# Second block's attention: each unit's z quarter in two halves around the turn of the weights

## Chip, cores and metric

One core of a Trainium2 chip. The metric is the device time of one execution in microseconds; the kernel before took 2187.45 us (median of three runs, 2185.56 to 2187.83).

## What is computed

A hybrid layer with a gated feed-forward network, and behind it a second block. All is float32, in 1024 positions of 1024 channels. Cut to what matters here:

```python
proj = h @ w_in                                   # h: normalized rows; z is its last 1024 columns
a_u, a_v, sq, sk, sv, mq, z = jnp.split(proj, split_at, axis=-1)
y_a = chunked_spatial_gating(gelu(a_u), gelu(a_v), ...)
y_b = sliding_window_attention(sq, sk, sv, attn_sinks, rel_bias)   # 4 heads of 64, blocks of 128 queries, 256 keys
y_c = memory_cross_attention(mq, mk, mv)                           # 4 heads of 64, 256 memory keys
y = jnp.concatenate([y_a, y_b, y_c], axis=-1) * jax.nn.silu(z)
x = x + rms_norm_2(y @ w_out, post_norm_g)
```

## The kernel before

The kernel is written by hand: each engine has its own instruction stream in a fixed order, and the streams meet at semaphores. Every product is made of three matmuls, for each float32 operand is split into a high and a low part (hi·hi, hi·lo, lo·hi). ScalarE makes the high part by a copy, VectorE or POOL the low part by a subtraction.

The attention of the second block is a loop over 16 **units** (`UNITS2`, L636): for each of 8 blocks of 128 queries first the sliding window (kind 0, even units), then the memory (kind 1, odd units). TensorE does in it four things:

- `logits2(n)` (L1615): 12 small matmuls into banks 1 and 2 or 4 and 5. It runs three units ahead, and waits until the exponentials of unit n-2 are done.
- `turn2(n)` (L1633): eight 128x128 transposes (L1639) of the normalized weights `p_s` into banks 6 and 7. It waits for `pn_done`, VectorE's normalization of unit n.
- `z_quarter(n)` (L1658): the projection z of 128 channels for 256 positions, 8 channel blocks of three matmuls (L1670), summed in bank 0. It waits for the weights' low part (`wlo_done`) and for the z copy of unit n-1 (`zcopy_done`), which empties bank 0. Its last matmul raises `lin_full`.
- `values2(n)` (L1642): 12 matmuls (L1655) into bank 3. It waits for `p2lo_done`, both low parts of the turned weights, and for `pvg_done`, the product that took unit n-1's values out of bank 3.

ScalarE's order in unit n (L2404): p_hi, the high parts of the turned weights (L2409); then `exps2(n + 2)`, four exponentials and, in even units, a fifth small one on `se` (L2375, L2379); then `z_copied(n)` (L2402), the copy of bank 0 to `z_s`; in odd units the silu over `z_s` (L2418). Exponential and silu need different tables, so a table load comes with each change. Behind every fourth unit ScalarE splits the next z weights (`w_hi`, L1721), and POOL subtracts their low part in four pieces (L3616).

VectorE's order in unit n (L3214): `maxima(n + 2)` (L3156 to L3167: a scale and bias, a maximum, two small operations `mx` and `nm`); p_lo (L3222); `gated_values(n - 1)` (L3208: two products into yz); in even units `z_product` (L3200); `sink_share`; `normed(n + 1)` (L3184 to L3189), which writes `p_s`.

After the loop, `y_high(0)` (L2395) on ScalarE, queued behind the last z copy, and `y_low(0)` (L3212) on VectorE give the first operands of the output product (L1692).

```python
for n in range(len(UNITS2)):
    if n >= 1:
        values2(n - 1)
    turn2(n)
    z_quarter(n)
    if n + 3 < len(UNITS2):
        logits2(n + 3)
```

Of the kernel before, what the change touches and what calls it, by code (L numbers as in the profile page):

```python
# [23 lines left out]
KD = D // P  # L24
# [140 lines left out]
def build(nc, I, out, scratch):  # L165
    PANELS, TILES = linear_plan()
    PANEL_AT = {key: p for p, key in enumerate(PANELS)}
    TILE_AT = {key: n for n, key in enumerate(TILES)}

    THROUGH = {p: max(n for (key, _), n in TILE_AT.items() if key == PANELS[p]) + 1 for p in range(len(PANELS))}  # L170
    WIDTH = {"wa": 512, "wc": 512, "poolw": 512}

# [4 lines left out]
    AT2 = {key: PB2 + n for n, key in enumerate(PANELS2)}  # L177
    TICK2 = {key: L2 + n for n, key in enumerate(TICKS2)}
    THROUGH2 = {key: max(n for (k_, _), n in TICK2.items() if k_ == key) + 1 for key in PANELS2 if (key, 0) in TICK2}
    UP_AT = {key: n for n, key in enumerate(UPPER)}  # L180

# [41 lines left out]
    with ExitStack() as ctx:  # L223
# [9 lines left out]
        def sem(name):  # L233
            return ctx.enter_context(nc.semaphore(name))
# [219 lines left out]
        whi_done, wlo_done, lin_full, pair_full = sem("whi_done"), sem("wlo_done"), sem("lin_full"), sem("pair_full")  # L454
# [46 lines left out]
        def tile_rows(r):  # L501
            return P if r < 8 else META
# [4 lines left out]
                       for half in range(2)]  # L507

        SCORES_TO = [sum(blk <= b for blk, _, _, _ in SCORES) for b in range(NB)]

        def scores_behind(kind, m, j, half):
# [58 lines left out]
        zs_done, ZS_0 = gate_done, 4 * KD  # L570
        zcopy_done, ZCOPY_0 = y_done, 4 * KD
# [70 lines left out]
        def key_chunks(n):  # L642
            return [1] if n == 0 else [0, 1]
# [388 lines left out]
        def _(pe):  # L1032
# [106 lines left out]
            for r in range(NB):  # L1139
                mm = pe.transpose(ps[:, b, 8 * r:8 * r + 8], w_row[32:40, P * r:P * r + P], ident[32:40, 32:40])  # L1140
# [35 lines left out]
            for m in range(4):  # L1176
                scored_product("u", m, FULL)
                if m == 2:

                    pe.wait_ge(cn_done, 1)  # L1180
                    for j, (t0, tiles, _) in enumerate(XGROUPS):
                        b = open_tile(TILE_AT[("ctok", 0), j])
                        for r in tiles:
                            mm = pe.transpose(ps[0:tile_rows(r), b, P * (r % 4):P * (r % 4) + P], c_sq[:, P * r:P * r + tile_rows(r)], ident[:, :])
# [411 lines left out]
            for n in range(2):  # L1596
                b = upper(("svt", n))
                for c in range(4):
                    mm = pe.transpose(ps[:, b, P * c:P * c + P], sv_f[:, BANK * n + P * c:BANK * n + P * c + P], ident[:, :])
# [15 lines left out]
            def logits2(n):  # L1615

                blk, kind = UNITS2[n]
                if n == 1:
                    pe.wait_ge(e2_done, E2_0 + 4)
                elif n == 2:  # L1620
                    pe.wait_ge(zs_done, ZS_0 + 7)
                elif n >= 3:
                    pe.wait_ge(e2_done, E2_0 + 4 * n - 4)
                q_parts, k_parts = ((mq_hi, mq_lo), (mk_hi, mk_lo)) if kind else ((sq_hi, sq_lo), (kd_hi, kd_lo))
                a, z = (0, MEM) if kind else (P * max(blk - 1, 0), P * blk + P)
                for c, (i, (x, y)), u in [(c, e, u) for c in range(2) for e in enumerate(((0, 0), (0, 1), (1, 0))) for u in range(2)]:
                        r0, h = DH * u, 2 * c + u
                        o = 2 * P * c + 2 * P - (z - a)
                        mm = pe.matmul(ps[:, logit_bank(n) + h % 2, o:o + z - a], q_parts[x][r0:r0 + DH, c, P * blk:P * blk + P],
                                       k_parts[y][r0:r0 + DH, c, a:z], start=i == 0, stop=i == 2)  # L1630
                mm.then_inc(lg_full, 1)

            def turn2(n):  # L1633
                pe.wait_ge(pn_done, PN_0 + 4 * n + 4)
                for kc in key_chunks(n):
                    if n >= 1 and (n - 1, kc) in TURN_AT:
                        pe.wait_ge(p2lo_done, P2LO_0 + TURN_AT[n - 1, kc] + 1)
                    for h in range(4):
                        mm = pe.transpose(ps[:, 6 + kc, P * h:P * h + P], p_s[:, n % 2, 2 * (h % 2) + h // 2, P * kc:P * kc + P], ident[:, :])  # L1639
                    mm.then_inc(pt_full, 1)  # L1640

            def values2(n):  # L1642
                blk, kind = UNITS2[n]
                if n >= 1:
                    pe.wait_ge(pvg_done, 2 * n)
                pe.wait_ge(p2lo_done, P2LO_0 + TURN_AT[n, 1] + 1)
                for c in range(2):
                    chunks = key_chunks(n)
                    for kc in chunks:
                        if kind:  # L1650
                            v_hi, v_lo = mv_hi[:, kc, P * c:P * c + P], mv_lo[:, kc, P * c:P * c + P]
                        else:
                            v_hi, v_lo = vd_hi[:, blk - 1 + kc, c, :], vd_lo[:, blk - 1 + kc, c, :]
                        for i, (a, r) in enumerate(((v_hi, p2_hi), (v_hi, p2_lo), (v_lo, p2_hi))):
                            mm = pe.matmul(ps[:, 3, 2 * P * c:2 * P * c + 2 * P], a, r[:, kc, 2 * P * c:2 * P * c + 2 * P],  # L1655
                                           start=kc == chunks[0] and i == 0, stop=kc == chunks[-1] and i == 2)
                mm.then_inc(pv_full, 1)

            def z_quarter(n):

                key, t0 = ("z", n // 4), 2 * P * (n % 4)
                p = AT2[key]
                pe.wait_ge(wlo_done, p + 1)
                if n == 0:
                    pe.wait_ge(zs_done, ZS_0 + 8)
                else:
                    pe.wait_ge(zcopy_done, ZCOPY_0 + n)
                for k in range(KD):
                    for i, (wt, r) in enumerate(((w_hi, x_hi), (w_hi, x_lo), (w_lo, x_hi))):
                        mm = pe.matmul(ps[:, 0, 0:2 * P], wt[:, p % 2, P * k:P * k + P], r[:, k, t0:t0 + 2 * P],  # L1670
                                       start=k == 0 and i == 0, stop=k == KD - 1 and i == 2)
                mm.then_inc(lin_full, 1)

            logits2(0)
            linear(("z", 7), 0, x_hi, x_lo, *HALF[0])
# [3 lines left out]
            for n in range(len(UNITS2)):  # L1679
                if n >= 1:  # L1680
                    values2(n - 1)
                turn2(n)
                z_quarter(n)
                if n + 3 < len(UNITS2):
                    logits2(n + 3)
            values2(len(UNITS2) - 1)
# [2 lines left out]
            def out_step(half, k, b):  # L1689
                hi, lo = out_weights(k)  # L1690
                for i, (y, w) in enumerate(((x_hi, hi), (x_lo, hi), (x_hi, lo))):
                    mm = pe.matmul(ps[:, b, :], y[:, k, P * b:P * b + P], w[:, half * BANK:half * BANK + BANK],  # L1692
                                   start=k == 0 and i == 0, stop=k == KD - 1 and i == 2)
                return mm

            for k in range(KD):
                pe.wait_ge(wlo_done, AT2["wout", k] + 1)
                pe.wait_ge(ylob_done if k % 2 else yloa_done, (YLOB_0 if k % 2 else YLOA_0) + k // 2 + 1)
                for b in ((0, 1, 2, 4, 5, 6, 7, 3) if k == 0 else range(NB)):
                    if k == 0 and b == 3:  # L1700
                        pe.wait_ge(pvg_done, 2 * len(UNITS2))
                    mm = out_step(0, k, b)
                    if k == KD - 1:
                        mm.then_inc(lin_full, 1)
            for b in range(NB):
                pe.wait_ge(wy_done, WY_0 + b + 1)
                for k in range(KD):
                    mm = out_step(1, k, b)
# [1974 lines left out]
```

## Time and profile before

| | us |
|---|---|
| median of three runs | 2187.45 (2185.56 to 2187.83) |
| the profiled execution | 2189.16 |
| its span | 2187.4 |
| TensorE matmul busy | 2150.4 (98%) |
| VectorE busy | 1407.0 (64%) |
| ScalarE busy | 910.5 (42%) |
| POOL busy | 1091.4 (50%) |
| mean granted TensorE clock | 0.997 |

The span is that of the instructions in the trace; the 1.8 us between it and the execution's time lie around it. The attention loop takes 1990.5 to 2088.3 of the span. Matmuls are pipelined: each lasts 0.28 us in the trace where the next starts 0.12 us behind it, so starts are compared below, not ends.

### The profile page before, as it was taken

Reading aid. Unit: us, or ns where it says so; the run is one execution under the profiler, and the core shown is the slowest. Engines: PE = TensorE matmul, PEld = TensorE weight load, DVE = VectorE, ACT = ScalarE, POOL = GpSimd, SP = SyncE. Lnnn points to the kernel's source line nnn. Section 1 sums busy time; section 2 is a strip of 40 time slices with the busy share of each in tenths; the row PEclk is TensorE's granted clock in tenths of the full one; section 3 lists DMA queues with packets and bytes.
Section 4 is the critical chain, followed back from the end, with each engine's and each line's share of the span. In section 5 each row is a group of like instructions: output and inputs, shape, how many; then the busy total and the mean of one; then the engine's idle time right before and its main releaser. Section 6 shows DMA issues by size and latency. Waiting matters only on the chain.

```text
span 2187.4 us, 29801 instructions
## 1 busy us (share of the span) xinstructions
PE 2150.4 (98%) x10520; PEld 1790.8 (82%) x10520; DVE 1407.0 (64%) x2799; ACT 910.5 (42%) x1618; POOL 1091.4 (50%) x859
## 2 busy tenths in 40 slices
PE   7999999999999999999999999999999999999998
PEld 6998788998888778887887878878888888888976
DVE  5256899999942567743677676766467746206934
ACT  5245522233225675433442232223446454227832
POOL 1388533465554344246655565656498624121173
PEclk9999999999999999999999999999999999999999
DMA  3632212111234222145525444344966331111131
GB/s 118 210 97 73 63 44 58 49 49 34 73 99 128 65 67 91 39 144 177 180 97 176 148 153 169 130 163 174 347 213 202 107 116 57 41 49 40 52 114 78
DMA packets 254103, 245.03 MB, mean 112 GB/s; under 512 B 11393, under 2 KB 195870, under 8 KB 253966
## 3 DMA queue, kind: packets, MB, share of 16 engines
q1 hardware_dynamic: 249808, 230.05, 32.6%
q10 hardware_dynamic: 4158, 13.16, 1.5%
q8 instruction: 85, 1.39, 0.3%
q14 instruction: 52, 0.43, 0.1%
HBM read 178.73 MB, written 63.25 MB: 111 GB/s over the span
## 4 chain that ended last, share of the span: by engine, by line
PE 90%; DVE 4%; ACT 2%; issue 2%; POOL 2%; DMA 0%; SPq 0%; ACTq 0%; DVEq 0%; POOLq 0%
PE ps L1052 31%; PE ps L1392 17%; PE ps L1416 9%; PE ps L1462 9%; PE ps L1244 6%; PE ps L1692 3%; PE ps L1359 2%; PE ps L1217 2%; PE ps L1283 2%; PE ps L1266 1%; PE ps L1113 1%; PE ps L1670 1%; PE ps L1150 1%; POOL wo_lo L3616 1%; PE ps L1515 1%
## 5 line engine op out<-in xcount | busy, mean ns | idle before, releaser
L3284 POOL TENSOR_TENSOR w_lo<-w_raw,w_hi 128x256 fp32r<-128x256 f32 (+2 forms) x271 | 309.4, 1164 | 532.7 <-ACT w_hi L1721 532.6
L1052 PE MATMUL ps<-x_hi,w_hi 128*128 128x512 f32 (+2 forms) x960 | 358.4, 373 | 1.0 <-ACT mix_s L1876 0.7
L1052 PE MATMUL ps<-x_lo,w_hi 128*128 128x512 f32 (+2 forms) x960 | 358.8, 374 | 0.0
L1052 PE MATMUL ps<-x_hi,w_lo 128*128 128x512 f32 (+2 forms) x960 | 357.1, 372 | 0.0
L1052 PEld LDWEIGHTS ps<-x_hi,w_hi 128*128 128x128 f32 x960 | 180.6, 188 | 31.7 <-POOL w_lo L3284 2.2
L1052 PEld LDWEIGHTS ps<-x_hi,w_lo 128*128 128x128 f32 x960 | 180.9, 188 | 28.6
L1052 PEld LDWEIGHTS ps<-x_lo,w_hi 128*128 128x128 f32 x960 | 180.4, 188 | 28.5 <-issue 0.2
L2598 DVE MATCH_REPLACE8 score<-best,score 128x400 f32<-128x400 f32 (+3 forms) x224 | 183.8, 821 | 0.0
L2594 DVE MAX8 best<-score 128x8 f32<-128x400 f32 (+3 forms) x224 | 180.4, 835 | 1.3
L1721 ACT CAST w_hi<-w_raw 128x1024 fp32r<-128x1024 f32 (+1 forms) x129 | 127.8, 991 | 103.2 <-PE ps L1052 68.1
L1416 PE MATMUL ps<-x_hi,wr_hi 128*128 128x512 f32 x380 | 138.5, 395 | 0.0
L1392 PE MATMUL ps<-x_hi,wr_hi 128*128 128x512 f32 x320 | 126.3, 395 | 1.1 <-DVE a L2934 1.1
L1392 PE MATMUL ps<-x_lo,wr_hi 128*128 128x512 f32 x320 | 127.0, 397 | 0.0
L1392 PE MATMUL ps<-x_hi,wr_lo 128*128 128x512 f32 x320 | 126.1, 394 | 0.0
L1416 PE MATMUL ps<-x_hi,wr_lo 128*128 128x512 f32 x308 | 121.5, 394 | 0.0
L1462 PE MATMUL ps<-x_hi,w_hi 128*128 128x512 f32 x272 | 109.8, 404 | 0.0
L1462 PE MATMUL ps<-x_lo,w_hi 128*128 128x512 f32 x272 | 108.2, 398 | 0.0
L1462 PE MATMUL ps<-x_hi,w_lo 128*128 128x512 f32 x272 | 107.6, 396 | 0.0
L2061 ACT CAST wr_hi<-rawg 128x512 fp32r<-128x512 f32 x83 | 51.5, 622 | 124.6 <-PE ps L1392 72.4
L1392 PE MATMUL ps<-xh_P,wr_hi 128*128 128x512 f32 x240 | 95.5, 398 | 0.5
L1392 PE MATMUL ps<-xh_P,wr_lo 128*128 128x512 f32 x240 | 94.6, 394 | 0.0
L1392 PE MATMUL ps<-xl_P,wr_hi 128*128 128x512 f32 x240 | 94.6, 394 | 0.0
(473 smaller groups left out, 5465.1 us busy)
## 6 DMA issues: line engine op xcount, KB each, us to landing
w_raw<-in_w_in SPq DMA_DIRECT2D x74, 512.0 KB, 3.7
wdr<-as_scratch SPq DMA_DIRECT2D x77, 256.0 KB, 3.8
rawg<-in_w_gate_up SPq DMA_DIRECT2D x22, 512.0 KB, 3.9
rawu<-in_w_gate_up SPq DMA_DIRECT2D x22, 512.0 KB, 5.3
wdr<-in_w_down SPq DMA_DIRECT2D x22, 512.0 KB, 3.8
as_scratch<-ac SPq DMA_DIRECT2D x44, 256.0 KB, 2.6
wt_scratch<-wdr SPq DMA_DIRECT2D x33, 256.0 KB, 4.8
as_scratch<-a SPq DMA_DIRECT2D x33, 256.0 KB, 2.6
```

Of the source, the lines that this page charges most:

```text
L1052: mm = pe.matmul(ps[:, b, 0:n], w[:, s, P * k:P * k + P], r[:, k, t0:t0 + n], start=k == 0 and i == 0, stop=k == kd - 1 and i == 2 and ext ...
L1217: mm = pe.matmul(ps[:, 4 + 2 * (n % 2) + ch, 0:w], a[:, blk % 2, 4 * hg + h, :], kk[:, k0 + ch * w:k0 + ch * w + w], start=i == 0, stop=i ...
L1244: mm = pe.matmul(ps[:, tile_bank(key, j), :], w[:, p % 2, P * k:P * k + P], r[:, k, t0:t0 + BANK], start=k == 0 and e == 0, stop=k == KD - ...
L1392: mm = pe.matmul(ps[:, b, :], w[:, q % SLOTS, P * k:P * k + P], xb(low, prod, k), start=k == 0 and e == 0 and first, stop=k == 3 and e == ...
L1416: mm = pe.matmul(ps[:, 4 * (p % 2) + f, :], w[:, (M2 + s) % SLOTS, P * f:P * f + P], sr(low, s), start=j == 0 and e == 0, stop=j == HJ - 1 ...
L1462: mm = pe.matmul(ps[:, lin_bank(key, j), 0:n], wt[:, p % 2, P * k:P * k + P], r[:, k, t0:t0 + n], start=k == 0 and i == 0, stop=k == KD - ...
L1692: mm = pe.matmul(ps[:, b, :], y[:, k, P * b:P * b + P], w[:, half * BANK:half * BANK + BANK], start=k == 0 and i == 0, stop=k == KD - 1 an ...
L1721: act.copy(w_hi[:, p % 2, 0:width(p)], w_raw[:, p % 2, 0:width(p)]).then_inc(whi_done, 1)
L2061: act.copy(wr_hi[:, q % SLOTS, :], block_source(q)).then_inc(wh_done, 1)
L2594: dve.max(out=best[:, a, :], in_=keys(blk)).then_inc(topk_step, 1)
L2598: dve.match_replace(out=keys(blk), in_to_replace=best[:, a, :], in_values=keys(blk), imm_value=SENT).then_inc(topk_step, 1)
L3284: low = pool.tensor_tensor(w_lo[:, p % 2, a:a + step], w_raw[:, p % 2, a:a + step], w_hi[:, p % 2, a:a + step], ALU.subtract)
```

## The change

The z quarter of every unit is cut into two halves of four channel blocks (12 matmuls). The first half, with both waits, stands ahead of the unit's turn; the second, with the increment of `lin_full`, behind it. The sum in bank 0 stays open over the transposes, which go to banks 6 and 7.

```diff
-            def z_quarter(n):
+            def z_quarter(n, k0):
                 key, t0 = ("z", n // 4), 2 * P * (n % 4)
                 p = AT2[key]
-                pe.wait_ge(wlo_done, p + 1)
-                if n == 0:
-                    pe.wait_ge(zs_done, ZS_0 + 8)
-                else:
-                    pe.wait_ge(zcopy_done, ZCOPY_0 + n)
-                for k in range(KD):
+                if k0 == 0:
+                    pe.wait_ge(wlo_done, p + 1)
+                    if n == 0:
+                        pe.wait_ge(zs_done, ZS_0 + 8)
+                    else:
+                        pe.wait_ge(zcopy_done, ZCOPY_0 + n)
+                for k in range(k0, k0 + KD // 2):
...
-                mm.then_inc(lin_full, 1)
+                if k0:
+                    mm.then_inc(lin_full, 1)
...
                 if n >= 1:
                     values2(n - 1)
+                z_quarter(n, 0)
                 turn2(n)
-                z_quarter(n)
+                z_quarter(n, KD // 2)
                 if n + 3 < len(UNITS2):
                     logits2(n + 3)
```

The order on TensorE before, from the last matmul of the values of unit 0 (`vd_lo` is their low part) over the turn of unit 1 to the start of its z quarter; a row's waits stand in brackets (`score_acc` is the semaphore of p_s, `ptlo_done` that of p_lo, `y_done` that of the z copy):

```order
L1655 MATMUL ps<-p_hi,vd_lo 128x256
L1639 MATMUL ps<-ident,p_s 128x128 [waits score_acc]
L1639 MATMUL ps<-ident,p_s 128x128 x3
L1639 MATMUL ps<-ident,p_s 128x128 [waits ptlo_done]
L1639 MATMUL ps<-ident,p_s 128x128 x3
L1670 MATMUL ps<-x_hi,w_hi 128x256 [waits y_done,wlo_done]
```

With the change, the same place, as far as the start of z:

```order
L1655 MATMUL ps<-p_hi,vd_lo 128x256
L1671 MATMUL ps<-x_hi,w_hi 128x256 [waits y_done,wlo_done]
L1671 MATMUL ps<-x_lo,w_hi 128x256
```

and the same turn, further on, between the two halves of z:

```order
L1671 MATMUL ps<-x_hi,w_lo 128x256
L1639 MATMUL ps<-ident,p_s 128x128 [waits score_acc]
L1639 MATMUL ps<-ident,p_s 128x128 x3
L1639 MATMUL ps<-ident,p_s 128x128 [waits ptlo_done]
L1639 MATMUL ps<-ident,p_s 128x128 x3
L1671 MATMUL ps<-x_hi,w_hi 128x256
```

The wait for the z copy stood behind the turn and is ahead of it now; the turn's own waits stay at its two groups of four transposes, and 12 of z's 24 matmuls have passed them. No row of ScalarE, VectorE, POOL or SP moves.

## Rows read from the trace of the kernel before

**Rows 1.** The page, busy time, share of the span and instructions of each engine.

```profile
PE 2150.4 (98%) x10520; PEld 1790.8 (82%) x10520; DVE 1407.0 (64%) x2799; ACT 910.5 (42%) x1618; POOL 1091.4 (50%) x859
```

**Rows 2.** Busy time in one period: stretch, length, PE, PEld, DVE, ACT, POOL, PEclk, DMA, GB/s.

```profile
1996.16:2021.48 25.32, 25.16 (x225) 23.89 (x225) 24.03 (x55) 20.97 (x55) 2.83 (x4) 1.00 0.11 35
```

**Rows 3.** The list of waits of TensorE, 1985 to 2095: total, times, longest.

```profile
PE ps L1692 <- DVE x_lo L3212: 1.3, 1, 1.3
PE ps L1639 <- DVE p_s L3189: 1.1, 5, 0.3
```

**Rows 4.** Order of time, TensorE: start, length, line, tile [idle before <- releaser].

```profile
1996.16 1.09 PE L1639 MATMUL ps<-ident,p_s 128*128 128x128 f32 x8 [0.34 <-DVE p_s L3189]
...
2002.45 1.04 PE L1639 MATMUL ps<-ident,p_s 128*128 128x128 f32 x8
...
2007.16 0.38 PE L1655 MATMUL ps<-p_hi,vd_hi 128*128 128x256 f32 x1
...
2008.68 1.04 PE L1639 MATMUL ps<-ident,p_s 128*128 128x128 f32 x8
...
2021.48 1.09 PE L1639 MATMUL ps<-ident,p_s 128*128 128x128 f32 x8 [0.16 <-DVE p_s L3189]
...
2072.12 1.09 PE L1639 MATMUL ps<-ident,p_s 128*128 128x128 f32 x8 [0.16 <-DVE p_s L3189]
...
2077.30 1.04 PE L1639 MATMUL ps<-ident,p_s 128*128 128x128 f32 x8
...
2082.99 1.09 PE L1639 MATMUL ps<-ident,p_s 128*128 128x128 f32 x8 [0.31 <-DVE p_s L3189]
```

**Rows 5.** The chain of waits, 1996 to 2010: start, length, what.

```profile
2003.49 2.84 PE ps L1670 x24
...
2009.32 0.59 ACT p_hi L2409
```

**Rows 6.** Order of time, POOL.

```profile
2015.93 2.83 POOL L3616 TENSOR_TENSOR w_lo<-w_raw,w_hi 128x256 fp32r<-128x256 f32 x4 [21.78 <-ACT w_hi L1721]
```

**Rows 7.** Order of time, ScalarE.

```profile
1991.21 0.59 ACT L2409 CAST p_hi<-ps 128x512 fp32r<-128x512 f32 x1
...
1994.22 0.47 ACT L2375 ACTIVATE p_s<-ps,nm 128x256 f32<-128x256 f32 x1 [1.12 <-DVE nm L3167]
...
1996.12 0.38 ACT L2402 COPY z_s<-ps 128x256 f32<-128x256 f32 x1
...
2003.09 1.07 ACT L2409 CAST p_hi<-ps 128x512 fp32r<-128x512 f32 x2 [0.64 <-PE ps L1639]
...
2007.38 0.38 ACT L2402 COPY z_s<-ps 128x256 f32<-128x256 f32 x1
...
2020.31 0.36 ACT L2402 COPY z_s<-ps 128x256 f32<-128x256 f32 x1
```

**Rows 8.** Order of time, VectorE, units 2 to 4.

```profile
2003.67 0.16 DVE L3165 TENSOR_TENSOR mx<-mx,sink 128x4 f32<-128x4 f32 x1
...
2003.95 1.29 DVE L3222 TENSOR_TENSOR p_lo<-ps,p_hi 128x512 fp32r<-128x512 f32 x2
2005.16 0.86 DVE L3208 TENSOR_TENSOR yz<-yz,ps 64x256 f32<-64x256 f32 x2
...
2009.94 1.29 DVE L3222 TENSOR_TENSOR p_lo<-ps,p_hi 128x512 fp32r<-128x512 f32 x2 [0.40 <-ACT p_hi L2409]
...
2016.14 0.55 DVE L3165 TENSOR_TENSOR mx<-mx,sink 128x4 f32<-128x4 f32 x1
...
2017.31 1.28 DVE L3222 TENSOR_TENSOR p_lo<-ps,p_hi 128x512 fp32r<-128x512 f32 x2
2018.51 0.85 DVE L3208 TENSOR_TENSOR yz<-yz,ps 64x256 f32<-64x256 f32 x2
```

**Rows 9.** Order of time, VectorE, unit 13.

```profile
2073.43 1.29 DVE L3222 TENSOR_TENSOR p_lo<-ps,p_hi 128x512 fp32r<-128x512 f32 x2
2074.64 0.86 DVE L3208 TENSOR_TENSOR yz<-yz,ps 64x256 f32<-64x256 f32 x2
```

## Prediction

> **What bounds the kernel now.** The change touches only the TensorE stream of the second block's attention, so I read the profile from the outside in. The page's busy rows come first [rows 1]: TensorE's matmul row is busy for 98% of the span, and VectorE for 64%. Averages over the span say little of one loop, so the next view is the busy time of one period of the loop, four units, from turn 1 to turn 5 [rows 2]; the next two read alike (25.32 us each). The reader is to see that TensorE is at 25.16 of 25.32 us, that VectorE is at 24.0, and that the granted clock is 1.00, the upper of its two levels (2.4 GHz). Two engines are within 5% of full there, not one. Third, the list of waits [rows 3]: TensorE waits in the whole loop 1.1 us, in five pieces, for the normalized weights p_s that a turn reads. That is all that a better place of the z work could save directly.
>
> Last, the order of events, which carries the sum. I call the start of unit n's turn T(n). From the TensorE rows [rows 4]: T2 is 2002.45, the values of unit 2 start at 2007.16 or T2+4.71, behind z and the logits, and T3 is 2008.68 or T2+6.23. Without a wait every unit takes this 6.23 us. T3 to T5 is 2021.48-2008.68 = 12.80 instead of 12.46, for T5 waited for p_s. The chain of waits shows one quarter's 24 matmuls as a piece of 2.84 us [rows 5], so half a quarter is 1.42 us. The 12 values matmuls, of the same shape, take 1.52 (2007.16 to 2008.68), so a switch from another kind of group costs up to 0.10.
>
> **What the change does.** No instruction is added or removed; 12 matmuls per unit go from behind the turn to ahead of it. Seen from the turn, the work behind it shrinks by 1.42 us, and the work ahead of it grows by as much. What the rest of the chip hangs on the turn is a chain: ScalarE copies the turned weights (p_hi), VectorE subtracts (p_lo), then VectorE multiplies the previous unit's values into yz and so frees the values' bank. The next values2 waits for both. And the first half's wait (the z copy of the unit before, which empties bank 0) is now ahead of the turn, which is queued behind it on TensorE, as are ScalarE's p_hi and VectorE's p_lo of that unit. No DMA is moved on any queue; the first half's other wait, for w_lo, is met long before: the weights of units 8 to 11 come from POOL's pass of 2015.93 [rows 6], in unit 4, and so it is with the others.
>
> *Term 1, even units without a weight split (2, 6, 10).* ScalarE runs without a gap from p_hi(2) at 2003.09 through a table load and four exponentials to the end of the z copy, 2007.38+0.38 = 2007.76 [rows 7], which is T2+5.31. The release takes some 0.04 us (p_hi's end at 2009.32+0.59 = 2009.91 [rows 5] to VectorE's start at 2009.94 [rows 8] is the like), so the first half of z(3) starts at T2+5.35 and T3 is T2+6.77 instead of T2+6.23: +0.54. The values' wait is hidden under it: yz is done at 2005.16+0.86 = T2+3.57 [rows 8], the values go at 3.61 instead of the 4.71-1.42 = 3.29 at which TensorE is there, take 1.52 (2008.68-2007.16) and end at T2+5.13, before 5.35. The Trainium skill's page Perfetto Trace Analysis, section Matmuls, advises that independent groups rotate through different PSUM banks, so that one's evacuation overlaps the next group; all z quarters share bank 0, and by that rule alone the sum would hold the z copy's wait and no other. That is the second rival.
>
> *Term 2, even units behind a weight split (4, 8, 12).* Here VectorE decides. From p_lo(3) at 2009.94, that is T3+1.26, it works without a gap to the end of yz in unit 4, 2018.51+0.85 = 2019.36 or T3+10.68 [rows 8]. From mx to p_lo, with the small operation nm between, it needs 1.17 us there (2016.14 to 2017.31) and 0.28 in unit 2 (2003.67 to 2003.95), for POOL's w_lo pass runs beside it from 2015.93 to 2018.76 [rows 6, 8]: 0.89 us more. I take this as staying: the pass would have to come over 1 us later or 1.5 us earlier against VectorE to miss both operations, and z(3), which sets off the split, is ready earlier by no more than 1.42. TensorE would reach the values at T4+3.29 = T3+9.52, and waits to 10.72. Then values 1.52 and first half 1.42: T5 is T3+13.66 instead of T3+12.80: +0.86. The old wait for p_s (0.34) is inside the 12.80. The z copy of unit 4 ends at 2020.31+0.36 = 2020.67, T3+11.99 [rows 7], under the values' end of 12.24, so it costs nothing more.
>
> *Term 3, odd units.* p_lo starts at T+1.31 in unit 13 (2073.43) and yz ends at 2074.64+0.86 = T13+3.38 [rows 9], so the values go at 3.42 instead of 3.29: +0.13, less 0.06 which a turn behind an idle stretch takes longer today (6.29 for T1 to T2). +0.07 for unit 1, 5, 9; in 3, 7, 11 it is covered by term 2's chain, which starts at T3.
>
> One period is so 0.54+0.86+0.07 = 1.47, and three periods (T1 to T13) 4.4 us.
>
> *Term 4, the start.* Turn 0 goes 1.42 later, and with it p_hi(0), from 1991.21 to 1992.63. Behind it ScalarE has 0.61 and a table load of 1.28, so its exponentials of unit 2 start at 1994.54 instead of 1994.22, and the z copy of unit 0 at 1996.44 instead of 1996.12 [rows 7]. It takes 0.38 and 0.04, then comes the half of z(1): T1 is 1998.28 instead of 1996.16: +2.1.
>
> *Term 5, the end.* From unit 13 on no logits lie between z and the values (T13 to T14 is 5.18, T14 to T15 5.69 [rows 4]). Behind T13 TensorE would be at the values by 5.18-1.42-1.42 = 2.34 and waits to 3.42; with 1.52 and 1.42 T14 is T13+6.36: +1.2. Behind T14 VectorE's p_lo at T+1.26 (as in unit 3) and 2.07 more (to the end of yz, as in unit 13 [rows 9]) free the values at 3.37, so T15 is T14+6.31: +0.6. From T15 on the last z quarter closes 1.42 earlier, and on it hang the z copy, x_hi, x_lo and the first output product, which today waits 1.3 for x_lo [rows 3], and still waits: the values of unit 15 end at T15+3.4+1.5 = 4.9, and x_lo is there at T15+5.18+1.3-1.42 = T15+5.1 (5.18 being a turn, a whole z and the values, as from T13 to T14): -1.4.
>
> **Sum**: 2.1+4.4+1.2+0.6-1.4 = +6.9 us. The output stage behind is shifted as a whole, for its stages hang on this z copy. The profiled execution took 2189.16 and becomes 2196.1; it stands 1.71 above the median of the runs shown, 2187.45, which becomes 2194.3.
>
> Unknown: what the one switch more per unit costs, for nothing like it stands in the trace: between 0 and 16 x 0.10 = 1.6. I take 0, as the first half of z follows values of its own shape, and keep the 1.6 for the range. Below, the terms could be too large if VectorE's chain shortens; rival three is that bound.
>
> **Rivals.** *One, not slower: the gap filler.* The first half fills TensorE's waits for p_s and nothing new is waited for: -1.1 us, 2186.4. It decides whether VectorE frees the values' bank by T+3.29 and ScalarE empties bank 0 by T+4.81. For it: all five waits of the loop are at this place [rows 3]. Against: the rows give 3.57 and 5.31 in unit 2.
>
> *Two: only bank 0 waits.* If yz frees the values in time, what is left is the start 2.1, 0.54 in unit 2, in unit 4 the copy's end T4+5.75 plus 0.04 and 1.42 against 6.56, so 0.65, less the 0.06 of a turn behind an idle stretch, three times 1.13, some 0.3 in unit 14, and -1.4: +4.4, 2191.8. Against it: yz's release is a row later than 3.29 in every unit.
>
> *Three: the small operations escape POOL.* If with the shift mx and nm miss the w_lo pass, the chain of term 2 is 0.89 shorter and the z copy decides: T5 is T3+6.23+6.77 = 13.00, +0.20 instead of +0.86, so -2.0 over three periods: +4.9, 2192.3. The Trainium skill's page SBUF — State Buffer, section Who interferes with whom, says that the port shared by VectorE and GpSimd is an exclusive lock, taken against VectorE operations with two SBUF inputs or in a two-port mode; the trace agrees (p_lo, with one PSUM input, takes 1.28 beside POOL and 1.29 without).
>
> *Four: more than I count*, each of 16 switches and of the 7 restarts of z behind its new wait costing the 0.10 of above: 1.6 to 2.3 us on top, 2195.9 to 2196.6.
>
> **How the numbers follow.** Forecast 0.62, rival one 0.05, two 0.09, three 0.09, four 0.15. The likeliest gives 2194.3. The range reaches from rival two less 1 us, for the spread of the runs (2185.56 to 2187.83 in three), to just above rival four: 2190.8 to 2197.0. It leaves out rival one and the tails. About 0.2% or 4.4 us is what a measurement can tell from no change, 2191.8 the border: half of rival two, all of one and a rest are within it, so same 0.14, faster 0.03, slower 0.83.
>
> **What would show it.** TensorE waits in the loop near 10 us instead of 1.1, with yz L3208 and z_s L2402 as releasers and p_s gone from the list; periods of 26.8 us instead of 25.32; a turn of unit 1 about 2.1 us later; the last z copy 2.5 us behind T15. VectorE's busy time per period unchanged at 24.0. Wrong if the periods stay at 25.3, if p_s is still the releaser, or if the granted clock in the loop is below 1.00.

## The result, and the profile after

The changed kernel takes 2193.95 us (median of eight runs, 2191.97 to 2196.39) against 2187.64 us of the kernel before (eight runs, 2185.06 to 2188.18). The ratio is 1.0031, with a 95% interval of 1.0023 to 1.0040: slower by 6.3 us. The forecast was +6.9 us and 2194.3.

The page's row of busy times, to be held against [rows 1]:

```profile
PE 2149.7 (98%) x10520; PEld 1787.0 (82%) x10520; DVE 1404.6 (64%) x2799; ACT 910.4 (42%) x1618; POOL 1090.8 (50%) x859
```

No figure has moved by more than 0.3%, as no instruction was added. The profiled span is 2191.9 us, only 4.5 more than before. That is not the change's doing: the loop begins at 1988.74 in this execution and at 1990.52 in the one before, behind 1990 us of the same instructions. Across all the kernels of this study that start lies between 1987.0 and 1992.0, so a profiled span is not fit to compare edits of 1 or 2 us. I compare the **loop**: from TensorE's first matmul behind logits 2 to the first output product. Behind it, both profiles are equal again, 89.96 us to the start of TensorE's last matmul.

The busy time by stretch, over that loop, the kernel before first (stretch, length, PE, PEld, DVE, ACT, POOL, granted clock, DMA share, GB/s):

```profile
1990.52:2089.67 99.15, 96.69 (x852) 92.01 (x851) 89.59 (x201) 77.05 (x195) 11.70 (x17) 1.00 0.20 71
```

and the changed kernel, the loop and then its three periods (turn 1 to 5, 5 to 9, 9 to 13), which answer to [rows 2]:

```profile
1988.74:2094.10 105.36, 97.89 (x852) 92.19 (x851) 88.52 (x201) 76.51 (x195) 11.75 (x17) 1.00 0.18 66
```

```profile
1996.73:2023.28 26.55, 25.42 (x227) 23.93 (x226) 23.26 (x53) 20.42 (x53) 2.85 (x4) 1.00 0.06 21
2023.28:2049.81 26.53, 25.40 (x227) 23.90 (x225) 23.70 (x55) 20.42 (x53) 2.85 (x4) 1.00 0.06 21
2049.81:2076.34 26.53, 25.40 (x226) 23.90 (x225) 23.70 (x55) 20.42 (x53) 2.85 (x4) 1.00 0.09 30
```

The loop is 6.21 us longer, which accounts for the difference of the medians (6.31). The granted clock is 1.00 in all rows, the level of 2.4 GHz, and each period is 1.21 to 1.23 us longer. TensorE's busy time grows by 0.24 to 0.26 us a period though its work is the same: the first matmul of z behind its wait is drawn 0.36 us long, and 0.28 is usual. VectorE's busy time, forecast unchanged at 24.0, is 23.26 to 23.70: `mx` behind the weight split takes 0.16 us instead of 0.55, which is taken up below. So neither row of busy times shows the loss; the list of waits does. TensorE's, from 1985 to 2100, against [rows 3]:

```profile
PE ps L1655 <- DVE yz L3211: 5.3, 9, 0.9
PE ps L1671 <- ACT z_s L2405: 1.8, 4, 1.1
```

The 1.1 us of waits for p_s at the turn are gone, as the change meant. The 1.3 us for x_lo are off the list too, but not quite gone: x_lo is done at 2093.95 and the first output product starts 0.15 us behind it, where the last matmul of the values has started at 2093.68. In their place stand two new ones at the places forecast: the values (L1655) wait for VectorE's product into yz, and the first half of z (L1671) for ScalarE's z copy. The list names 7.1 us in 13 pieces, less than the 10 forecast; its row for the weight loads ahead of the values has 8.5 us in 15 pieces, so the short waits are missing in it.

TensorE in order of time, changed kernel, against [rows 4]:

```profile
1995.23 0.35 PE L1671 MATMUL ps<-x_hi,w_hi 128*128 128x256 f32 x1 [1.14 <-ACT z_s L2405]
...
1996.73 1.03 PE L1639 MATMUL ps<-ident,p_s 128*128 128x128 f32 x8
...
2003.05 1.04 PE L1639 MATMUL ps<-ident,p_s 128*128 128x128 f32 x8
...
2006.59 0.39 PE L1655 MATMUL ps<-p_hi,vd_hi 128*128 128x256 f32 x1 [0.20 <-DVE yz L3211]
...
2008.51 0.36 PE L1671 MATMUL ps<-x_hi,w_hi 128*128 128x256 f32 x1 [0.24 <-ACT z_s L2405]
...
2010.00 1.04 PE L1639 MATMUL ps<-ident,p_s 128*128 128x128 f32 x8
...
2023.28 1.03 PE L1639 MATMUL ps<-ident,p_s 128*128 128x128 f32 x8
```

ScalarE in unit 2, against [rows 7]:

```profile
2007.98 0.38 ACT L2405 COPY z_s<-ps 128x256 f32<-128x256 f32 x1
```

VectorE around unit 4, against [rows 8], and the POOL pass beside it, against [rows 6]:

```profile
2011.25 1.29 DVE L3225 TENSOR_TENSOR p_lo<-ps,p_hi 128x512 fp32r<-128x512 f32 x2 [1.20 <-ACT p_hi L2412]
...
2017.46 0.16 DVE L3168 TENSOR_TENSOR mx<-mx,sink 128x4 f32<-128x4 f32 x1
2017.65 0.60 DVE L3170 TENSOR_SCALAR nm<-mx 128x4 f32<-128x4 f32 x1
2018.17 1.27 DVE L3225 TENSOR_TENSOR p_lo<-ps,p_hi 128x512 fp32r<-128x512 f32 x2
2019.37 0.86 DVE L3211 TENSOR_TENSOR yz<-yz,ps 64x256 f32<-64x256 f32 x2
```

```profile
2016.77 2.85 POOL L3619 TENSOR_TENSOR w_lo<-w_raw,w_hi 128x256 fp32r<-128x256 f32 x4 [24.39 <-ACT w_hi L1724]
```

Here is the chain that the forecast used. Turn 2 at 2003.05, z copy done at 2007.98+0.38 = 2008.36 = T2+5.31 (forecast 5.31), first half of z at 2008.51, turn 3 at 2010.00 = T2+6.95. From p_lo(3) at T3+1.25 VectorE works without a gap to the end of yz, 2020.23 = T3+10.23 (forecast 10.68). The difference of 0.45 is at mx and nm: 0.71 us from mx to p_lo instead of the 1.17 of before, though POOL's pass lies over both operations.

### The profile page after: what moved, and what is told of

Read it like the earlier page. It is cut to its first block, busy times and chain, and to the rows that moved or that the text cites. A ratio compares the mean times of both kernels' runs of the same rounds, so it can differ in the third digit from the quotient of the medians.

```text
span 2191.9 us, 29801 instructions
## 1 busy us (share of the span) xinstructions
PE 2149.7 (98%) x10520; PEld 1787.0 (82%) x10520; DVE 1404.6 (64%) x2799; ACT 910.4 (42%) x1618; POOL 1090.8 (50%) x859
## 3 DMA queue, kind: packets, MB, share of 16 engines
q8 instruction: 85, 1.39, 0.3%
## 4 chain that ended last, share of the span: by engine, by line
PE 90%; DVE 4%; ACT 2%; issue 2%; POOL 2%; DMA 1%; SPq 0%; ACTq 0%; DVEq 0%; POOLq 0%
PE ps L1052 31%; PE ps L1392 17%; PE ps L1416 9%; PE ps L1462 9%; PE ps L1244 6%; PE ps L1695 3%; PE ps L1359 2%; PE ps L1217 2%; PE ps L1283 2%; PE ps L1266 1%; PE ps L1671 1%; PE ps L1113 1%; PE ps L1150 1%; PE ps L1655 1%; POOL wo_lo L3619 1%
## 5 line engine op out<-in xcount | busy, mean ns | idle before, releaser
L3467 POOL TENSOR_TENSOR wr_lo<-rawg,wr_hi 128x512 fp32r<-128x512 f32 x42 | 68.6, 1634 | 52.3 <-ACT wr_hi L2064 52.3
```

The lines of the kernel that those rows point to most:

```text
L3467: pool.tensor_tensor(wr_lo[:, q % SLOTS, :], block_source(q), wr_hi[:, q % SLOTS, :], ALU.subtract).then_inc(wl_even, 1)
```

## The experiments

Theory A is mine: two new waits, of z for bank 0 and of the values for yz, and the longer of the two sets each unit. Theory B: bank 0 alone. Theory C: the cut itself costs (a switch more per unit). There are eleven variants. For each stands the busy row over its loop; its second number is the loop's length. Each loop length is that of one execution, and how far it repeats from one execution to the next was not measured; equal units within a loop mostly agree to 0.05 us. e1, e2, e5, e6, e8 and e9 have only this one execution, so their whole times are not compared. "Unit n" is from turn n to turn n+1.

**e1, z copy early**, on the changed kernel. ScalarE's even units:

```diff
                 for h in range(4):
+                    if h == 3 and n >= 2 and n % 2 == 0:
+                        z_copied(n - 2)
                     src = ps[:, logit_bank(n) + h // 2, ...]
...
-                z_copied(n)
+                if n % 2 or n + 2 >= len(UNITS2):
+                    z_copied(n)
```

> The changed kernel with one edit on ScalarE: in even units the z copy stands between the third and the fourth exponential instead of behind the last. Loop length means: from TensorE's first matmul behind logits 2 to the first output product; 99.15 us before, 105.36 with the change. Theory A (two new waits, z for bank 0 and the values for yz, which partly hide each other): the wait for z_s goes, turn 1 comes 0.5 us earlier, units 2, 6, 10 shorten from 6.95 to about 6.6, the others stay, for there the values' wait binds: loop about 103.6. Theory B (bank 0 alone is the cause): the loop falls to about 100. Theory C (the cut itself costs, a switch more per unit, and the waits are incidental): 105.4 as it was.

The loop, then TensorE's waits, then VectorE and POOL in unit 4:

```profile
1990.42:2095.53 105.11, 96.95 (x853) 91.74 (x851) 90.45 (x201) 76.81 (x195) 11.66 (x17) 1.00 0.18 66
```

```profile
PE ps L1655 <- DVE yz L3214: 7.3, 9, 1.3
PE ps L1671 <- ACT z_s L2407: 0.6, 1, 0.6
```

```profile
2018.11 0.75 DVE L3171 TENSOR_TENSOR mx<-mx,sink 128x4 f32<-128x4 f32 x1
2018.89 0.66 DVE L3173 TENSOR_SCALAR nm<-mx 128x4 f32<-128x4 f32 x1
2019.46 1.27 DVE L3228 TENSOR_TENSOR p_lo<-ps,p_hi 128x512 fp32r<-128x512 f32 x2
```

```profile
2017.40 2.82 POOL L3622 TENSOR_TENSOR w_lo<-w_raw,w_hi 128x256 fp32r<-128x256 f32 x4 [23.35 <-ACT w_hi L1724]
```

Turn 1 came 0.55 us sooner and units 2, 6, 10 took 6.44 to 6.49 instead of 6.95 to 6.97, as theory A has it. But units 4, 8, 12 took 7.50 to 7.56 instead of 6.96, and the loop fell by 0.25 us only; my expectation of 103.6 missed. The loss is between mx and p_lo, 1.35 us here and 0.71 in the changed kernel. I took up a third cause: VectorE's small operations held up by POOL's pass.

**e2, yz first**, on the changed kernel. VectorE's loop:

```diff
+                if n >= 1:
+                    gated_values(n - 1)
                 for kc in key_chunks(n):
...
-                if n >= 1:
-                    gated_values(n - 1)
```

> The changed kernel with one edit on VectorE: the products into yz of the unit before stand ahead of p_lo instead of behind it, so in odd units they fall into VectorE's wait for p_hi. Theory A: the values no longer wait for yz in odd units and at the end; T13 to T15 falls from 12.55 to about 10.9; in even units the z copy still binds, so a period stays near 26.4: loop about 103.6. Theory B: the wait is for bank 0, loop 105.4. Theory C: 105.4.

```profile
1987.11:2090.49 103.38, 97.63 (x852) 92.32 (x851) 87.05 (x201) 76.39 (x195) 13.13 (x17) 1.00 0.19 67
```

```profile
PE ps L1671 <- ACT z_s L2405: 4.2, 7, 1.1
PE ps L1695 <- DVE x_lo L3215: 0.9, 1, 0.9
PE ps L1655 <- DVE p_lo L3227: 0.7, 3, 0.3
```

103.38 against 103.6 expected; period 26.33, T13 to T15 11.19. Theories B and C had 105.4. The values' wait for yz is gone, and what stays is z behind the copy of the even units, seven times: 4.2 us instead of 1.8. In the even units nothing was gained (6.95 to 6.96 us as before): there the wait for the z copy had hidden the one for yz.

**e3, both edits** on the changed kernel.

> Both edits together on the changed kernel (z copy ahead of the fourth exponential in even units, yz ahead of p_lo). Theory A: the two waits hide each other, so the edits together bring far more than the sum of each alone (3.5): a period near 25.0 and the loop near 99.2, as before the change. Theory B: as with the copy alone, near 100. Theory C: about 105 still; if the added switch costs 0.1 a unit, 1.6 us stay above 99.15.

```profile
1987.01:2086.59 99.58, 97.39 (x853) 92.32 (x851) 87.08 (x201) 76.59 (x195) 13.13 (x17) 1.00 0.19 70
```

99.58 against 99.2. With both waits out of the way the loop is back near its 99.15, which theory C does not give; theory B had e3 near 100 too, but not e2. Alone, the two edits took 0.25 and 1.98 us off the loop; together 5.78. That gap is not a measure of how far the two waits hide each other, though: most of it is the POOL pass that e1 ran into and that mx and nm miss in e2 and e3 (0.28 us there from mx to the operation behind nm), as e8 shows below. (In whole time, ten runs: 2187.2 against 2186.52, ratio 1.0003, 0.9993 to 1.0012. So it is no slower any more, and no faster.) Even units still take 6.41, 0.2 more than odd ones. The trace says what holds them: in unit 2 the last matmul of the values starts at 2005.33, the z copy ends at 2005.43, and the first half of z starts at 2005.57 instead of 0.12 behind the values. It is so in units 2 to 12, so the z copy still comes a little late.

**e4, two blocks ahead** of the turn and six behind, on the changed kernel (`z_quarter` takes its last block too):

```diff
-                z_quarter(n, 0)
+                z_quarter(n, 0, 2)
                 turn2(n)
-                z_quarter(n, KD // 2)
+                z_quarter(n, 2, KD)
```

> The changed kernel, but with two channel blocks (6 matmuls, 0.71 us) ahead of the turn and six behind it. Theory A: TensorE comes to the values at T+4.0 and to z at T+5.5, later than yz (3.6) and the z copy (5.4) are there but behind the weight split (4.5), so nearly no wait is left: period 24.95 to 25.1, turn 1 some 0.8 later than before the change, loop about 98.8, 0.3 to 0.5 below the kernel before, which still waits for p_s. Theory C: the cut costs what it costs wherever it stands: 105.4. A cost by matmul moved would give 102.3.

```profile
1987.23:2087.51 100.28, 96.63 (x853) 91.99 (x851) 89.80 (x201) 76.73 (x195) 11.69 (x17) 1.00 0.19 69
```

VectorE in units 4 and 12, and POOL in unit 4 and 12:

```profile
2014.07 0.76 DVE L3168 TENSOR_TENSOR mx<-mx,sink 128x4 f32<-128x4 f32 x1
2014.87 0.67 DVE L3170 TENSOR_SCALAR nm<-mx 128x4 f32<-128x4 f32 x1
...
2065.39 0.16 DVE L3168 TENSOR_TENSOR mx<-mx,sink 128x4 f32<-128x4 f32 x1
2065.59 0.60 DVE L3170 TENSOR_SCALAR nm<-mx 128x4 f32<-128x4 f32 x1
```

```profile
2013.39 2.82 POOL L3619 TENSOR_TENSOR w_lo<-w_raw,w_hi 128x256 fp32r<-128x256 f32 x4 [22.52 <-ACT w_hi L1724]
...
2064.70 2.85 POOL L3619 TENSOR_TENSOR w_lo<-w_raw,w_hi 128x256 fp32r<-128x256 f32 x4 [22.83 <-ACT w_hi L1724]
```

100.28, 1.5 above my 98.8, yet far below both numbers of theory C. Turn 1 came 1.3 us later than in the kernel before instead of 0.8. Units 1 to 12 took 6.21 to 6.26, as a unit without waits does, but for units 4 and 8, which took 6.96 and 6.94. Unit 12 of the same kernel took 6.25. The rows show why: mx starts 0.68 us behind the pass in unit 4 and takes 0.76, and 0.69 behind it in unit 12 and takes 0.16. (In whole time, ten runs: ratio 1.0008, 0.9999 to 1.0018.)

**e5, cut in even units only**, on the changed kernel:

```diff
-                z_quarter(n, 0)
+                if n % 2 == 0:
+                    z_quarter(n, 0, KD // 2)
                 turn2(n)
-                z_quarter(n, KD // 2)
+                z_quarter(n, KD // 2 if n % 2 == 0 else 0, KD)
```

> The changed kernel with the cut only in even units (in odd ones the whole z quarter stands behind the turn, as before the change). Theory A: the z copy of an odd unit is early and costs nothing, but the values of the even unit come 1.42 us sooner after its turn and wait for yz (free at T+3.6, behind a weight split later): T(even) to T(odd) 5.2 or more instead of 4.8, T(odd) to T(even) 7.65; a period 26.2 to 26.7, turn 1 not later than before the change; loop 103.3 to 104.2. Theory B (bank 0 alone): the copy that is late is that of the even units, and nothing waits for it here: loop near 99.2. Theory C (the cut costs as such): half of 6.2 us, loop 102.2.

```profile
1987.84:2090.85 103.01, 97.62 (x852) 91.77 (x851) 89.77 (x201) 77.17 (x195) 11.63 (x17) 1.00 0.19 68
```

```profile
PE ps L1639 <- DVE p_s L3193: 3.0, 8, 0.4
```

**e6, cut in odd units only**, the same with `n % 2 == 1`.

> The changed kernel with the cut only in odd units. Theory A: z(odd) waits for the copy of the even unit only at the start (unit 1), later TensorE comes to it after 5.4; the values of odd units come by T+3.3 and wait 0.1, those of even units are late enough; a period 25.8 to 26.1, loop 101.8 to 102.6. Theory B: all of the loss is here, loop near 105. Theory C: 102.2.

```profile
1989.43:2092.44 103.01, 97.59 (x853) 91.81 (x851) 89.20 (x201) 76.39 (x195) 11.74 (x17) 1.00 0.19 67
```

Both loops are 103.01, so theory B (99.2 and 105) is out. For theory A e5 is 0.3 below its span, and e6 0.4 above, with a unit 8 of 8.91 us where mx met the pass (1.37 us from mx to p_lo, and 0.71 in units 4 and 12). That 3.86 and 3.86 add up to 7.7, not to 6.2, speaks against a fixed price per cut (2 x 3.1), if not strongly. In e6 the list has 4.0 us for yz in five pieces and 0.8 for z_s in one. I had the mechanism of e5 wrong: its list has a single entry for yz, 0.9 us, but eight waits for p_s at the odd turns. The late turn of an even unit makes p_hi and so p_lo and p_s late; the next turn comes 1.42 us sooner, as no z stands ahead of it, and waits.

**e7, POOL's pass moved**, on the kernel before the change:

```diff
                 p = AT2["z", m] + 2
+                if m in (7, 0, 1, 2):
+                    pool.wait_ge(nm2_done, NM2_0 + (4 if m == 7 else 4 * m + 8))
```

> The kernel before the change, with one edit on POOL: the low pass of the z weights in the loop waits for the maxima of an odd unit (nm of unit 3, 7, 11, 15 in VectorE's order), and so runs beside VectorE's idle time, p_lo and yz instead of beside mx and nm. If mx and nm are held up by POOL's pass (0.89 us in units 4, 8, 12, 0.6 in unit 0), they take 0.16 and 0.17 everywhere, the waits for p_s in turns 1, 5, 9, 13 go, periods fall from 25.32 to 24.95 and the loop from 99.15 to 97.7. If they are slow there for another reason (the mask of data, a queue), nothing moves: 99.15. If VectorE's other operations are held up in their place, periods stay at 25.3.

The loop, TensorE's waits, VectorE in unit 4 and POOL's pass, now in unit 5:

```profile
1989.60:2086.87 97.27, 95.70 (x852) 91.51 (x851) 88.20 (x201) 76.91 (x195) 11.72 (x17) 1.00 0.19 68
```

```profile
PE ps L1692 <- DVE x_lo L3212: 1.3, 1, 1.3
PE ps L1639 <- DVE p_s L3189: 0.2, 1, 0.2
```

```profile
2014.80 0.16 DVE L3165 TENSOR_TENSOR mx<-mx,sink 128x4 f32<-128x4 f32 x1
2014.99 0.17 DVE L3167 TENSOR_SCALAR nm<-mx 128x4 f32<-128x4 f32 x1
2015.07 1.29 DVE L3222 TENSOR_TENSOR p_lo<-ps,p_hi 128x512 fp32r<-128x512 f32 x2
```

```profile
2020.74 2.83 POOL L3616 TENSOR_TENSOR w_lo<-w_raw,w_hi 128x256 fp32r<-128x256 f32 x4 [21.89 <-DVE nm L3158]
```

The same two operations on the same data take 0.16 and 0.17 us once the pass runs elsewhere, the gap from mx to p_lo is 0.27 to 0.28 in all even units, the period falls from 25.32 to 24.81 to 25.00, and the loop to 97.27 (97.7 expected). So the 1.1 us of waits for p_s that the change was aimed at came from VectorE being held up by POOL. The pass now lies over another small operation, `rs` (0.48 us in unit 5 instead of 0.16), and no wait in TensorE's list answers to it: the 0.2 us left for p_s are at turn 15, where the kernel before waited 0.31. The whole time does not show the 1.9 us: 2186.81 (eleven runs) against 2186.61, ratio 1.0000, 0.9991 to 1.0009. A gain of 1.9 us would be 0.9991, at the edge of that interval, so the whole time neither confirms nor excludes it.

**e8, z copy early and POOL's pass moved**: the edits of e1 and e7 on the changed kernel.

> The copy-early kernel (cut in all units, z copy ahead of the fourth exponential) with the same edit on POOL. With the copy early alone units 4, 8, 12 took 7.55 us, for mx and nm fell on POOL's pass in a worse place (1.37 us from mx to p_lo instead of 0.71). Theory A: with the pass moved, all even units take the 6.49 of units 2, 6, 10; period 25.6 instead of 26.6, loop 105.11 - 3.2 = 101.9; the rest to 99.15 is the values' wait for yz. Theory B: bank 0 alone decided and is out of the way already, units 4, 8, 12 stay at 7.5.

```profile
1991.97:2093.82 101.85, 96.91 (x853) 91.70 (x851) 86.68 (x201) 76.58 (x195) 11.66 (x17) 1.00 0.18 67
```

```profile
PE ps L1655 <- DVE yz L3214: 4.0, 9, 0.9
```

101.85 against 101.9; even units from 2 to 12 took 6.42 to 6.50. This closes e1: its missing gain was taken by the pass. It also puts e3 right. With the pass out of the way the early z copy is worth 105.36-101.85 = 3.51 us, e2's edit 1.98, the sum 5.49, and both together gave 5.78. So the two waits hide little of each other, some 0.3 us. (The changed kernel with the pass moved and nothing else was not run. An estimate from its rows: in unit 4 the z copy ends at 2021.25+0.38 = 2021.63, with the release of 0.15 z could start at 2021.78, and it starts at 2021.81, so the pass alone holds it by 0.03 us.) And as 101.85 is still 2.7 above 99.15 with bank 0 free early, theory B is out here too.

**e9, two blocks ahead and POOL's pass moved**: the edits of e4 and e7.

> The kernel with two blocks ahead of the turn and six behind (loop 100.28, units 4 and 8 6.96, for mx and nm fell on POOL's pass and the values waited for yz), now with POOL's pass moved behind the maxima of odd units. Theory A (the cut costs nothing where neither the values nor z come before yz and the z copy): units 4, 8, 12 fall to 6.2 to 6.25 as the others, the start comes up to 0.35 sooner: loop 98.3 to 98.6, that is the start's and the end's terms above the 97.27 of the uncut kernel with the same POOL edit. Theory C (each cut costs a switch of 0.1): even units of 6.3 and more, loop 99.5 and above.

```profile
1989.86:2088.40 98.54, 96.59 (x852) 92.15 (x851) 87.52 (x201) 76.41 (x195) 11.69 (x17) 1.00 0.18 66
```

98.54, units 1 to 12 took 6.22 to 6.25. From unit 4 on they average 6.24, and units without a cut average 6.20 in e7 and 6.24 in e11, so a sum held open in bank 0 over a turn costs between nothing and 0.04 us a cut. (The odd units of e2 and e3, cut in halves, take 6.21.) Theory C with its 0.1 us a cut is out.

**e10, all three edits on the two-block cut**: those of e1, e2, e4 and e7.

> All three edits (z copy ahead of the fourth exponential, yz ahead of p_lo, POOL's pass moved) on the kernel with two blocks ahead of the turn. Theory A: nothing of the loop waits any more, period 24.8, the start is 0.5 sooner than with two blocks alone, T13 to T15 10.6 to 11.2: loop 97.2 to 97.9; no better than the uncut kernel with POOL's pass moved (97.27), since TensorE's own work sets the pace in both. Theory C: 98.8 and more.

```profile
1987.77:2084.68 96.91, 95.59 (x853) 91.88 (x851) 86.02 (x201) 76.50 (x195) 11.67 (x17) 1.00 0.19 68
```

The list of waits holds one entry in the loop, 1.3 us for x_lo at its end. The whole time is 2185.08 against 2186.8, ratio 0.9990, 0.9981 to 1.0000.

**e11, z whole in units 0 to 14, cut in unit 15 alone, POOL's pass moved**: on the changed kernel with the edit of e7,

```diff
-                z_quarter(n, 0)
+                c = KD // 2 if n == len(UNITS2) - 1 else 0
+                if c:
+                    z_quarter(n, 0, c)
                 turn2(n)
-                z_quarter(n, KD // 2)
+                z_quarter(n, c, KD)
```

> The best version that the runs point to: z whole behind the turn in units 0 to 14, cut in two halves around the turn in unit 15 alone, where it lets the last z copy end 1.4 us sooner after the turn, and POOL's pass moved. Theory A: loop as in the uncut kernel with POOL's pass moved (97.27), T14 to T15 longer by 1.1, T15 to the output product shorter by 1.45: 96.9. Against the kernel before, that is 2.2 us less in the loop, at the edge of what a measurement of the whole time can tell.

```profile
1988.71:2085.80 97.09, 96.02 (x852) 91.92 (x851) 87.99 (x201) 76.90 (x195) 11.69 (x17) 1.00 0.18 66
```

97.09: unit 14 longer by 1.05, T15 to the output product shorter by 1.47, but its periods are 0.1 longer than e7's. The whole time is 2184.64 (eleven runs) against 2186.8, ratio 0.9990, 0.9981 to 0.9999. By their medians e10 and e11 are so some 2 us faster than the kernel before, and by the ratios (1.0031 and 0.9990) some 8 to 9 us faster than the changed one. Against the kernel before the intervals end at 1.0000 and 0.9999, and 0.1% is below what I took as tellable; the other sign is the loop, 2.1 to 2.2 us shorter in one profile each.

## Why the prediction was right

The direction, the size and the places of the waits came out. That the sum is off by 0.7 us only is in part luck: term 2 was 1.1 us too large over its three units, and term 1 and the start together 0.8 too small. Each term by the profile:

| term | forecast us | measured us |
|---|---|---|
| start, turn 1 against the loop's start | +2.1 | 7.99-5.64 = +2.35 |
| units 2, 6, 10 (term 1) | +0.54 each | 6.95-6.23 = +0.72 |
| behind the weight split, T3 to T5 (term 2) | +0.86 each | 13.28-12.80 = +0.48 |
| units 1, 5, 9 (term 3) | +0.07 each | 6.29 to 6.32 against 6.29: 0 to +0.03 |
| three periods | +4.4 | +3.65 |
| T13 to T14, T14 to T15 | +1.2, +0.6 | +1.12, +0.56 |
| T15 to the output product | -1.4 | -1.47 |
| sum | +6.9 | +6.2 |

*Term 1 and the start* were 0.2 us too small each, 0.18 of it for one reason: I took 0.04 us from the end of ScalarE's copy to TensorE's start, from a release of VectorE by ScalarE. It is 0.15 (2008.36 to 2008.51), and the half quarter behind a wait takes 1.49 instead of 1.42.

*Term 2* is the step that was most mis-sized. I kept the 0.89 us of the POOL pass, arguing that the pass would still cover both operations. It does, and yet the price was 0.43 (0.71-0.28), for mx took its usual 0.16 us; by the rows in the last section it slipped in between two of POOL's four instructions. With 0.43 in place of 0.89 VectorE's chain and the z copy tie, and unit 4 takes 6.97 as unit 2 does. Rival three, that the price goes, was so half true: mx escaped the pass and nm did not. The runs show the price in the same place of the same loop as 0.28, 0.71, 1.17 and 1.35 to 1.39 us from mx to p_lo.

*Term 5* held to 0.1 us, and e2 showed its cause: with yz ahead, T13 to T15 falls from 12.55 to 11.19.

*Rivals one, two and four.* The gap filler is out by the list of waits, and e7 shows that the gap it would have filled had another cause. Bank 0 alone is out by e2, e5, e6 and e8. The switch that I left at nothing costs at most 0.04 us (e9), so of rival four only the restarts behind a wait are left, 0.07 each (1.49 against 1.42).

What the text on record left out: an edit that removes one wait also moves VectorE against POOL's pass, and that can outweigh the wait. Term 1 said that in unit 2 the z copy's wait hides the values', and e2 bears it out (no gain in even units). But the sum of the two single edits, 0.25 (e1) and 1.98 (e2) against 5.78 together, misses its mark for another reason: with the pass moved the first is 3.51 (e8).

## What to carry to other kernels

When work is moved ahead of a step that another engine's chain hangs on, list what that engine must have done by the moved time at both ends: here 1.42 us of TensorE work ahead of the turn put two consumers' deadlines 1.42 us closer, and in a loop where two engines are within 5% of full that is paid at once. Before filling a gap, ask what made the engine in front late; here it was a third engine's pass lying over two operations of 4 elements, and moving that pass by one semaphore took 1.9 us off the loop in the profile (e7), where the fill could have brought 1.1 at most. The whole time did not show it. Compare such edits by the stretch that they touch, not by the span, which moved by up to 5 us ahead of the loop for the same instructions.

## What was unexpected of the hardware

In this loop VectorE's two small operations on SBUF, mx and nm, mostly end where the POOL instruction beside them ends, so their price depends on the phase. In unit 4 of the kernel before, POOL's first two pieces end at 2016.67 and 2017.37, mx at 2016.69 and nm at 2017.40. One of POOL's four instructions of a pass takes 0.73 to 0.77 us in the changed kernel:

```profile
L3619 POOL TENSOR_TENSOR w_lo<-w_raw,w_hi x28: 730/738/765, 1954.0 to 2071.9; 128x256 fp32r<-128x256 f32 x28
```

mx (two SBUF inputs of 128x4) takes 0.16 us where POOL is idle; 0.55 where it starts 0.21 behind the pass (before); 0.16 at 0.69 (changed kernel, and e4's unit 12); and 0.76 at 0.68 (e4's unit 4), 0.75 at 0.71 (e1). So the same operation costs 0.16 or 0.76 for starts that the trace puts within 0.03 us of each other: as I read it, it either slips in between two instructions of POOL or sits one out. POOL's rows bear this out: where mx takes 0.16, the second piece takes 0.77 us instead of 0.74 (2017.46 in the changed kernel, 2065.39 in e4), and the pass 2.85 instead of 2.82; where mx takes 0.76 (e4's unit 4), that piece runs its 0.74 from 2014.08 and mx ends with it. nm, behind it, has one SBUF input and takes 0.60 to 0.67 instead of 0.17 in all these cases. Operations with one input in PSUM (p_lo, yz, the large scale and bias, which lies over a pass in unit 0) are the same to 0.02 us with and without the pass. The Trainium skill's page SBUF — State Buffer, section Who interferes with whom, calls the shared port an exclusive lock held for the whole instruction; the durations above agree. It also goes the other way: where mx and nm come first, as in e3, a POOL pass of four takes longer:

```profile
2013.84 3.31 POOL L3622 TENSOR_TENSOR w_lo<-w_raw,w_hi 128x256 fp32r<-128x256 f32 x4 [23.19 <-ACT w_hi L1724]
```

against 2.83 in the kernel before. The whole of it is in the fourth piece, which starts 0.04 us behind VectorE's z product, an operation with two SBUF inputs:

```profile
2015.92 1.23 POOL L3622 TENSOR_TENSOR w_lo<-w_raw,w_hi 128x256 fp32r<-128x256 f32 x1
```

```profile
2015.88 0.68 DVE L3206 TENSOR_TENSOR yz<-yz,z_s 128x512 f32<-128x512 f32 x1
```

That the z product is the cause is the reading that fits; no run took it away to test it.
